# Opening of a four-layer diffusion step: modulation weights laid out by input tile, and the first two feed-forward steps multiplied tile by tile

## The reference, cut to what matters

```python
def modulate(x, g, shift, scale):
    return rms_norm(x, g) * (1 + scale) + shift
def modulation(cond, w, b):
    return jnp.split(jax.nn.silu(cond) @ w + b, N_MOD, axis=-1)
def half_ffn(x, shift, scale, gate, g, w_gu, w_down):
    h = modulate(x, g, shift, scale)
    a, u = jnp.split(h @ w_gu, 2, axis=-1)
    return x + FFN_RES * gate * ((jax.nn.silu(a) * u) @ w_down)
```

## Time and profile before

| what | value |
|---|---|
| median of the runs | 2907.52 us |
| the profiled execution | 2907.79 us, its span 2905.4 us |
| PE (matmul) busy | 2881.7 us (99%) |
| DVE busy | 2306.3 us (79%) |
| ACT busy | 1303.7 us (45%) |
| DMA | 490.21 MB, mean 169 GB/s |
| granted TensorE clock | 1.0 of full speed |

### The profile page before, as it was taken

One profiled execution on the slowest core, in us unless ns is written; L12 is line 12 of the kernel. 1 busy time (PEld: TensorE's weight loads), 2 busy tenths in 40 slices (PEclk: granted clock), 3 DMA queues, 4 the chain that ended last, 5 costly groups with the idle time before them and its releaser, 6 DMA issues.

```text
span 2905.4 us, 44384 instructions
## 1 busy us (share of the span) xinstructions
PE 2881.7 (99%) x17542; PEld 2801.2 (96%) x17542; DVE 2306.3 (79%) x3489; ACT 1303.7 (45%) x2055; POOL 155.3 (5%) x164
## 2 busy tenths in 40 slices
PE   8999999999999999999999999999999999999999
PEld 6999979999999998999999998899999999989999
DVE  6999988888887887888888777788888887778553
ACT  4332564443443366443444348644334434664432
POOL 0000210000000030000000012000000001310000
PEclk9999999999999999999999999999999999999999
DMA  7666314455455522555455531254545555324342
GB/s 295 215 213 230 128 47 176 186 197 215 176 193 195 212 69 89 186 190 214 182 191 200 199 122 56 86 199 182 204 189 197 186 218 186 109 75 185 120 150 88
DMA packets 87865, 490.21 MB, mean 169 GB/s; under 512 B 11840, under 2 KB 13184, under 8 KB 51648
## 3 DMA queue, kind: packets, MB, share of 16 engines
q1 hardware_dynamic: 83840, 480.42, 44.6%
q0 software_dynamic: 3904, 8.24, 1.1%
HBM read 485.33 MB, written 3.29 MB: 168 GB/s over the span
## 4 chain that ended last, share of the span: by engine, by line
issue 72%; PE 24%; DVE 2%; DMA 1%; ACT 1%; POOL 0%; DVEq 0%; POOLq 0%; ACTq 0%
PE ps L936 5%; PE ps L884 4%; PE ps L903 2%; PE ps L889 2%; PE ps L1215 1%; PE ps L1131 1%; PE ps L907 1%; PE ps L1066 1%; DMA boot<-in_mod_w 1%; PE ps L1106 1%; PE ps L1051 1%; PE ps L1047 0%; PE ps L973 0%; PE ps L1151 0%; PE ps L977 0%
## 5 line engine op out<-in xcount | busy, mean ns | idle before, releaser
L884 PE MATMUL ps<-h_hi,w_hi 128*128 128x386 f32 x2688 | 907.9, 338 | 0.0
L884 PE MATMUL ps<-h_lo,w_hi 128*128 128x386 f32 x2688 | 892.6, 332 | 0.0
L1750 DVE TENSOR_TENSOR w_lo<-w_raw,w_hi 128x2048 fp32r<-128x2048 f32 (+4 forms) x280 | 700.7, 2503 | 33.3 <-ACT w_hi L1379 33.1
L1777 DVE CUSTOM_DVE_ANT_0 F_junk<-F_slab,cond,mod_b 128x1024 f32<-128x1024 f32 x544 | 706.6, 1299 | 13.6 <-DVE mod L1777 1.0
L1379 ACT ACTIVATE w_hi<-w_raw 128x2048 fp32r<-128x2048 f32 (+3 forms) x273 | 566.4, 2075 | 11.1 <-DMA w_raw<-in_ffn_dn 9.4
L884 PEld LDWEIGHTS ps<-h_lo,w_hi 128*128 128x128 f32 x2688 | 512.7, 191 | 0.0
L884 PEld LDWEIGHTS ps<-h_hi,w_hi 128*128 128x128 f32 x2688 | 502.7, 187 | 0.0
L889 PE MATMUL ps<-h_hi,w_lo 128*128 128x386 f32 x2688 | 493.6, 334 | 0.0
L903 PE MATMUL ps<-F_act_hi,w_hi 128*128 128x384 f32 x1408 | 475.6, 338 | 0.0
L903 PE MATMUL ps<-F_act_lo,w_hi 128*128 128x384 f32 x1408 | 470.8, 334 | 0.0
L889 PEld LDWEIGHTS ps<-h_hi,w_lo 128*128 128x128 f32 x2688 | 468.2, 187 | 0.0
(11 more groups left out here) (421 smaller groups left out, 3576.2 us busy)
## 6 DMA issues: line engine op xcount, KB each, us to landing
w_raw<-in_ffn_gu SPq DMA_DIRECT2D x175, 1024.0 KB, 4.8
F_slab<-in_mod_w SPq DMA_DIRECT2D x272, 512.0 KB, 5.6
w_raw<-in_ffn_dn SPq DMA_DIRECT2D x64, 1408.0 KB, 6.4
w_raw<-in_d_w SPq DMA_DIRECT2D x8, 1536.0 KB, 6.9
boot<-in_mod_w SPq DMA_DIRECT2D x8, 1024.0 KB, 7.9
w_raw<-in_a_w SPq DMA_DIRECT2D x4, 1536.0 KB, 6.8
w_raw<-in_b_w SPq DMA_DIRECT2D x4, 1536.0 KB, 6.5
w_raw<-in_c_w SPq DMA_DIRECT2D x8, 544.0 KB, 3.5
```

What stands on the lines that cost most here:

```text
L884: pe.matmul(ps[:, 2 * par + u, 0:N_MOVE], w[0][:, k, u, :], h[:, k, :], start=(k == 0 and h is h_hi), stop=False)
L1750: dve.tensor_tensor(w_lo[par][:, 0:w], w_raw[par][:, 0:w], w_hi[par][:, 0:w], ALU.subtract).then_inc(w_split_lo.sem, 1)
L1777: dve.tensor_tensor_reduce(out=junk[:], in0=w, in1=cond[:, c, :], scale=scale, scalar=mod_b[:, n:n + 1], op0=ALU.mult, op1=ALU.add, accum_ ...
```

## The change

Piece m of the modulation weights now holds all 1024 input channels for 128 output columns of shift and 128 of scale, that is everything that tile m of `h` needs. When it lands, PE makes its rows in eight matmuls of 256 columns (`rows_of_modulation`), ACT copies them out (`copy_rows`), PE turns them with two small matmuls (`turn_modulation`), DVE makes shift and scale of tile m (`first_modulation`), ACT and DVE make `h_hi` and `h_lo` of tile m. PE multiplies tile m-2 into step 0 and tile m-3 into step 1 between the rows and the turn of piece m. Both chunks are loaded before piece 2. The plan gives no slab to step 0.

```diff
+BOOT_W = BOOT_PARTS * P
+B_BOOT, B_BOOT_TURNED = (4, 6), 5
...
-            steps = [1] * 3 + [2, 1, 1] * 6 + [1] + [3] * 5 + [2] * 2 + [0]
+            steps = [0, 1, 2, 1] + [2, 1, 1] * 6 + [3] * 5 + [2] * 2 + [0]
...
             def load_boot(i):
-                if i >= BOOT_FLIGHT:
-                    sp.wait_ge(boot_landed[i - BOOT_FLIGHT], 16)
+                if i >= 3:
+                    sp.wait_ge(boot_landed[i - 2], 16)
...
+            sp.dma_start(x[:], a["x"]).then_inc(x_in, 16)
...
-            sp.wait_ge(boot_landed[5], 16)
+            sp.wait_ge(boot_landed[0], 16)
             sp.dma_start(w_raw[0][:, 0:half], w_dram["gu"][0][:, 0:half]).then_inc(first_half_landed, 16)
-            sp.wait_ge(boot_landed[6], 16)
+            sp.wait_ge(x_in, 16)
             sp.dma_start(w_raw[0][:, half:GU_CHUNK], w_dram["gu"][0][:, half:GU_CHUNK]).then_inc(w_landed[0], 16)
+            load_boot(1)
+            sp.wait_ge(first_half_landed, 16)
+            load_w(CB[0], 1, GU_CHUNK, w_dram["gu"][1])
+            for i in range(2, KD):
+                load_boot(i)
...
+            def rows_of_modulation(m):
+                pe.wait_ge(boot_landed[m], 16)
+                for k in range(KD):
+                    q = 32 * (k % 4)
+                    mm = pe.matmul(ps[q:q + 32, B_BOOT[m % 2], 0:BOOT_W], cond_t[:, k, :],
+                                   boot[m][:, k * BOOT_W:(k + 1) * BOOT_W], start=(k < 4), stop=(k >= 4))
+                mm.then_inc(boot_made, 1)
+            def turn_modulation(m):
+                pe.wait_ge(boot_rows_ready, m + 1)
+                for t in range(BOOT_PARTS):
+                    at = 2 * (BOOT_PARTS * m + t)
+                    mm = pe.matmul(ps[:, B_BOOT_TURNED, at:at + 2], boot_rows[m % 2][:, t * P:(t + 1) * P],
+                                   cond_of_rows[:], start=True, stop=True)
+                mm.then_inc(boot_turned, 1)
+            def gu_part(j, k):
...
+                pe.wait_ge(h_ready.sem, h_ready.after(0, k))
+                for u in range(2):
+                    for i, (lh, rh) in enumerate(((w[0], h_hi), (w[1], h_hi), (w[0], h_lo))):
+                        mm = pe.matmul(ps[:, 2 * j + u, 0:N_MOVE], lh[:, k, u, :], rh[:, k, :],
+                                       start=(k == 0 and i == 0), stop=(k == KD - 1 and i == 2))
...
+                for m in range(KD):
+                    rows_of_modulation(m)
+                    if m >= 2:
+                        gu_part(0, m - 2)
+                    if m >= 3:
+                        gu_part(1, m - 3)
+                    turn_modulation(m)
+                    if m == 0:
+                        stay_busy(3, B_WARM_BOOT)
+                    if m == KD - 2:
+                        stats(0)
+                gu_part(0, KD - 2)
+                broadcast(0)
+                gu_part(1, KD - 3)
+                gu_part(0, KD - 1)
+                gu_part(1, KD - 2)
+                gu_part(1, KD - 1)
...
+            def first_hi(m):
+                act.wait_ge(boot_modulated, m + 1)
...
+            for m in range(2, KD):
+                copy_rows(m)
+                if m in (2, 3):
+                    first_square(2 * m)
+                    first_square(2 * m + 1)
+                first_hi(m)
...
+            split_lo(CB[0], 1, GU_CHUNK)
+            for m in range(2, KD):
+                first_modulation(m)
+                if m in (2, 3):
+                    for n in range(2 * m, 2 * m + 2):
+                        add_squares(-1, n, n % 2)
+                first_lo(m)
+                if m == KD - 2:
+                    inverse_rms(0)
```

More of the change, by code:

```diff
@@ L575, in build @@
         boot = tiles["F"]["boot"]
-        boot_rows = junk[:, 0:BOOT_W]
+        boot_rows = [junk[:, i * BOOT_W:(i + 1) * BOOT_W] for i in range(2)]
         mixer_loads = {
@@ L672, in _ @@
                         if c or s:
-                            if s == 0 and c == 1:
-                                for n in range(BOOT_PARTS * KD, BOOT_PARTS * KD + LATE_SLABS):
+                            if s == 0 and c == 2:
+                                for n in range(BOOT_PARTS * KD, SLABS[0][1].start):
                                     load_slab(n)
@@ new lines, in turn_modulation @@
+            def turn_modulation(m):
[6 more added lines that the diff above has]
+            def gu_part(j, k):
+                h_hi, h_lo = input_of(0)
+                w = [q[j][:, 0:GU_CHUNK].rearrange("p (k u c) -> p k u c", k=KD, u=2) for q in (w_hi, w_lo)]
+                if j == 0 and k == 0:
+                    pe.wait_ge(first_half_hi, 1)
+                    pe.wait_ge(first_half_lo, 1)
+                elif j == 1 and k == 0 or j == 0 and k == KD // 2:
+                    pe.wait_ge(w_split_hi.sem, w_split_hi.after(0, j))
+                    pe.wait_ge(w_split_lo.sem, w_split_lo.after(0, j))
+                pe.wait_ge(h_ready.sem, h_ready.after(0, k))
[3 more added lines that the diff above has]
+                                       start=(k == 0 and i == 0), stop=(k == KD - 1 and i == 2))
+                if k == KD - 1:
+                    mm.then_inc(w_used.sem, 1)
@@ L1250, in boot_rows_of_modulation @@
-                stay_busy(1, B_WARM_BOOT)
-            def gu_zero():
-                h_hi, h_lo = input_of(0)
[L1256 to L1275, removed]
-                                       start=False, stop=(k == KD - 1))
-                mm.then_inc(w_used.sem, 1)
@@ L1622, in _ @@
             act.wait_ge(x_in, 16)
-            squares()
-            act.wait_ge(boot_made, 1)
-            act.activation(boot_rows, ps[:, B_BOOT[0], 0:BOOT_W], ACT.Copy).then_inc(boot_rows_ready, 1)
+            first_square(0)
+            first_square(1)
             act.wait_ge(first_half_landed, 16)
@@ L1628, in _ @@
             act.activation(w_hi[0][:, 0:half], w_raw[0][:, 0:half], ACT.Copy).then_inc(first_half_hi, 1)
-            for m in range(KD):
-                next_hi(0, m)
-                if m == 3:
-                    act.wait_ge(w_landed[0], landed(0))
-                    act.activation(w_hi[0][:, half:GU_CHUNK], w_raw[0][:, half:GU_CHUNK],
-                                   ACT.Copy).then_inc(w_split_hi.sem, 1)
+            first_hi(0)
+            act.wait_ge(w_landed[0], landed(0))
+            act.activation(w_hi[0][:, half:GU_CHUNK], w_raw[0][:, half:GU_CHUNK], ACT.Copy).then_inc(w_split_hi.sem, 1)
+            first_square(2)
+            first_square(3)
+            copy_rows(1)
+            first_hi(1)
+            split_hi(CB[0], 1, GU_CHUNK)
+            for m in range(2, KD):
[4 more added lines that the diff above has]
+                first_hi(m)
             for s in range(N_STAGE):
```

121 lines of the change are left out of this document (59 added, 62 removed).

## The result

The changed kernel takes 2912.62 us, the median of 19 runs (2910.66 to 2914.38), against 2907.57 us (2907.30 to 2908.85, 19 runs) before on the same chip. The ratio is 1.0017, with an interval of 1.0010 to 1.0023: 5.05 us more, which is within the 0.2% that I called no change, but above my range (2905.9 to 2911.2) and 4.7 us from the forecast of 2907.9. The profiled execution took 2911.86 us, its span 2909.4. Its runs also scatter over 3.7 us, those of before over 1.6.

A forecast was written before the change was run, and what follows sets the result against it. PE was taken to pace the first feed-forward stage, so step 2's start decides: 51.00 against 50.59 us, +0.4, the rest at nothing; 2907.79 became 2908.2, less 0.27 to the median: 2907.9 us, range 2905.9 to 2911.2.

The forecast's parts named there:

- T2: Landing of piece 2, put at 21.95 us (21.2 to 22.7), with a queue gap of 0.75 us.
- round of piece 2: PE's work on piece 2: rows 1.00, one tile of one step 1.07, turn 0.46, together 2.53 us.
- five rounds, stats, last turn: PE's rounds of pieces 3 to 7 at 3.59 us each, plus stats at 0.69 us.
- turn to `h_lo` of tile 7: After tile 7's turn, shift and scale 0.35, ACT's copy to DVE's first h_lo 1.10, h_lo 0.69: 2.14 us.
- slab pair: DVE's two reductions of the first slab, after tile 7's h_lo and ahead of step 0's sums: 2.54 us.
- `sq<-ps,rbc` to step 2: From DVE's start on step 0's sums, through SiLU, to the end of w_hi and step 2: 3.20 us.
- the clock falls: Rival: little PE work before piece 2 brings half speed back, costing 2.3 us; chance 0.25.
- rival 1: The rival that the clock falls before piece 2 lands: 2910.2 us, chance 0.25.
- PE sets the pace: From piece 3 on a round costs PE 3.59 us while pieces arrive every 2.49 us, so pieces wait for PE.
- The hand-over: Step 0's sums to step 2's w_hi comes into the open; PE idles some 2.0 us, step 2 starts at 51.00.
- DVE's margin: In steps 2 to 6 DVE finishes w_lo at least 1.5 us before PE asks, so its later start costs nothing.
- The run behind the opening: Everything after step 2's start was taken to move with it, at no further gain or loss.

The follow-up runs named there:

- e5: The changed kernel with six fillers behind the turn of piece 0 (three before), three behind that of piece 1 and two before step 2: 2909.59 us.
- e3: The changed kernel with two filler matmuls in PE's wait before step 2: 2911.14 us.
- e10: The changed kernel with the two columns of cond_of_rows taken from the existing tile junk, so that no new tile shifts addresses: 2915.35 us.
- e11: e5 without SP's wait for x ahead of the second half of chunk 0: 2908.86 us.
- e8: e5 with three pieces in flight instead of two: 2909.61 us.
- e7: The changed kernel with only step 0 between pieces, step 1 and its chunk behind, pieces 0 and 1 before x, three in flight, fillers before piece 2: 2907.16 us.
- e6: e5 with the first slab moved behind DVE's taking out of step 0's sums, and one filler before step 2 instead of two: 2908.37 us.
- e1: The kernel before with one unused tile of two float32 columns allocated where the changed kernel has cond_of_rows: 2904.90 us.
- e2: The changed kernel with three more fillers behind the turn of piece 1: 2913.52 us.
- e12: e9 with one filler matmul between the rows and the turn of piece 1: 2903.52 us.
- e9: e7 without the five fillers behind the turn of piece 1: 2903.77 us.

## Why the prediction was wrong, step by step

The terms stand against the profiled execution of after. T2 counts from the landing of piece 2.

| step of the prediction | forecast | measured | off, us |
|---|---|---|---|
| T2, piece 2 lands | 21.95 | 24.08 | +2.1 |
| round of piece 2 | 2.53 | 4.43 | +1.9 |
| five rounds, stats, last turn | 18.64 | 19.05 | +0.4 |
| turn to `h_lo` of tile 7 | 2.14 | 2.23 | +0.1 |
| slab pair | 2.54 | 2.53 | 0 |
| `sq<-ps,rbc` to step 2 | 3.20 | 3.24 | 0 |
| step 2 to the first dn sum, more than before | 0 | 1.6 | +1.6 |
| the rest of the run | 0 | -2.5 | -2.5 |

These add up to 3.6; with the 0.4 that was forecast, 4.0 is the difference between the spans. The median of after lies another 0.8 above its profiled execution, that of before 0.2 below its own.

1. **The failing step is the clock.** The sum has no term for it. I gave "the clock falls" a chance of 0.25, at 2.3 us; the round of piece 2 lost 1.8 (4.43 us, and 2.59 in e5), and the medians of e3 and e5 lie 1.6 apart. My argument against it, that rows and turn break the stretch, was false: with 1.7 us of work since 16.75 us the clock fell at 21.3, just before the idle stretch that I had named began. My price rested on the first rows of before (1.61 us against 1.06), read as a slow stretch of 4.7 us from PE's start; in after PE starts at 7.51 and the rows at 11.09 already take 1.07, so that stretch is not a fixed one. I had also written down an idle of 2.0 us before step 2, forecast correctly (2.21), and never asked the same question of it. It cost 1.5 us, shown by e3. With neither fall the same division takes 2909.59 us (e5). The Trainium skill, "TensorE: Matmul & The Clock Gate", section "Why this matters for your kernels", warns of idle gaps between bursts of matmuls. The trace of after agrees (2.21 us idle, clock 0.61 and 0.54 in the windows of 2 us behind 55), that of e10 doesn't (2.17 us idle, 1.00 behind it); rival 1, at 2910.2 us, was still nearer than my forecast.
2. **T2 was mis-sized by 2.1 us.** I had seen the wait for `x` and priced its gap at 0.75 us, at most 1.5. It came to 2.9 (24.08 against 21.2), outside my bounds: the four low slices hold 1.4 us of it. e11 shows that the wait is the cause: without it piece 2 lands at 21.35 us. Why a queue that stands dry for a while costs more than the bytes of its low slices stays open. Piece 0's rows, 0.8 us later than before through `ident`, delayed nothing.
3. **PE sets the pace: right.** 3.67 us a round against 3.59; e8 brings the pieces earlier and leaves the rounds at 3.67, e7 takes step 1's share out and the rounds fall to 2.60.
4. **The hand-over: right in size** (slab pair 2.53, eviction to step 2 3.24). e6 shows that 1.0 to 1.2 us of it were there for the taking.
5. **DVE's margin: right.** No wait of PE for `w_lo` follows in the first 420 us.
6. **The run behind the opening: wrong by 2.5 us to the good.** I took all that follows as unchanged. A tile of two columns moved the tiles behind it, and the dn matmuls changed their pace; e1 and e10 show it in both directions.

Two errors thus had the sign "slower" and one "faster". Had the layout not helped, the time would have been 2915.35 (e10), 0.24% above before. That the result stayed within the 0.2% that I had called no change is luck, and so is a distance of only 4.7 us from the forecast: the misses before the first dn sum add up to 6.1.

## What to carry to other kernels

When a kernel is bound by PE, list every idle stretch of PE that the new order makes, the short ones at hand-overs too, and charge each with the half-speed matmuls behind it; fillers help only if they end before the work that they wait for, so size them by the landing and re-size them when it moves. Products taken up as pieces land are worth something only for what PE would otherwise not do in that time: here step 1's share made each round 1 us longer and its chunk held piece 2 back, and the kernel that left it out (and brought the first pieces ahead of `x`) was faster. And run the kernel before with the new allocations alone, since a shift of addresses can be as large as the effect that is studied.

## What the runs showed of the hardware that I had not expected

- A matmul's mean changes with where the tiles lie: with one more tile of 8 bytes per partition ahead of them, `F_act_hi` by `w_hi` took 336 instead of 338 ns and `F_act_lo` by `w_hi` 335 instead of 334, 2.3 us of busy time and 2.65 us between the medians (e1; e10 shows the way back). The gu groups did not change.
- Behind a wait of 2.21 us the granted clock was 0.61 and 0.54 in the windows of 2 us from 55 on, and PE worked for 3.4 us before it was back (after). Behind a wait of 2.17 us at the same place it stayed at 1.00 (e10), and behind one of 2.18 us PE worked at full speed for 1.4 us before it fell (e2, step 2 from 57.78 us, granted 1.00 in 58 to 59 and 0.59 in 59 to 60). In the opening a gap of 1.30 us (e12) or 1.62 us (e9), after an uneven stretch, went ahead of a fall too, in some executions and not in others. The window row of 10 to 15 us shows 1.00 in e9 and 0.82 in e7 with the same code up to there.
- A blocked issue shows in the landings late and long: SP issued again from 11.11 us on, and the four slices from 11.25 to 14.25 us stayed under 300 GB/s. Without the block piece 2 landed 2.6 us earlier and the last load of a piece went out 2.1 us earlier than in e5 (e11), more than the 1.4 us that the missing bytes stand for.
